# Two GpSimd operations per weight unit, and a first sub-layer put in another order

## What is computed

```python
mx = jnp.split((jax.nn.silu(c) @ mod_w[l] + mod_b[l])[:, None, :], N_MOD, axis=-1)
x = x + 0.5 * mx[2] * swiglu(modulate(rms_norm(x, norm_ffn1[l]), mx[0], mx[1]), ffn1_w_in[l], ffn1_w_out[l])
ux = modulate(rms_norm(x, norm_mix[l]), mx[3], mx[4])
yx, yh = token_mixer(ux, uh, w_in[l], ..., not last)
x = x + mx[5] * yx
x = x + 0.5 * mx[8] * swiglu(modulate(rms_norm(x, norm_ffn2[l]), mx[6], mx[7]), ffn2_w_in[l], ffn2_w_out[l])
```

## Time and profile before

| | |
|---|---|
| median of 3 executions | 2095.47 us |
| lowest and highest | 2094.98 and 2096.15 us |
| the profiled execution | 2095.26 us |
| its span in the trace | 2093.5 us |
| mean granted clock of TensorE | 0.983 |
| TensorE busy | 2016.0 us (96%) |
| GpSimd busy | 937.9 us (45%) |
| VectorE busy | 859.4 us (41%) |
| ScalarE busy | 672.1 us (32%) |
| moved by DMA | 278.89 MB, 133 GB/s in the mean |

### The profile page before, as it was taken

How to read it: one execution, slowest core, us unless ns; L and a number is a source line. 1 busy time by engine, 2 the same in 40 slices (tenths; PEclk the granted TensorE clock), 3 DMA queues, 4 the chain that set the end, 5 groups by cost and what they waited for, 6 DMA issues and landing times.

```text
span 2093.5 us, 30142 instructions
## 1 busy us (share of the span) xinstructions
PE 2016.0 (96%) x10678; PEld 1646.4 (79%) x10678; DVE 859.4 (41%) x1320; ACT 672.1 (32%) x1063; POOL 937.9 (45%) x423
## 2 busy tenths in 40 slices
PE   4899999999999999999999999999999899989998
PEld 2677777887667888878877887788778777989998
DVE  5323123438763124633123345322334775574313
ACT  3222222234453223421222243222223444444333
POOL 2244434453112443344434344444434433867886
PEclk7999999999999999999999999999999999999999
DMA  8354665243112333444455235534533522655564
GB/s 288 126 189 134 215 202 168 69 107 120 45 41 60 90 100 91 131 160 150 121 161 167 71 114 162 181 108 141 170 112 93 145 76 66 180 151 151 165 181 127
DMA packets 436977, 278.89 MB, mean 133 GB/s; under 512 B 25219, under 2 KB 398461, under 8 KB 436653
## 3 DMA queue, kind: packets, MB, share of 16 engines
q1 hardware_dynamic: 401868, 206.79, 33.5%
q10 hardware_dynamic: 34944, 71.05, 9.6%
q0 software_dynamic: 96, 0.16, 0.0%
HBM read 276.92 MB, written 1.05 MB: 133 GB/s over the span
## 4 chain that ended last, share of the span: by engine, by line
PE 82%; issue 7%; DVE 5%; POOL 4%; DMA 1%; ACT 1%; ACTq 0%; POOLq 0%; SPq 0%; DVEq 0%
PE bank L1194 25%; PE bank L1195 24%; PE bank L1196 24%; POOL w_lo L421 4%; PE bank L1264 3%; DVE u_lo L866 1%; PE bank L1515 1%; PE bank L1450 1%; PE bank L1272 1%; PE bank L1497 1%; DVE tmp L853 1%; DMA tok_rows<-in_ctx 0%; PE bank L1397 0%; DMA dft_tok<-in_c_dft_tok 0%; DVE rstd L1024 0%
## 5 line engine op out<-in xcount | busy, mean ns | idle before, releaser
L421 POOL TENSOR_TENSOR w_lo<-w_raw,w_hi 128x1024 fp32r<-128x1024 f32 (+2 forms) x412 | 935.3, 2285 | 1143.1 <-ACT w_hi L453 1143.1
L1194 PE MATMUL bank<-u_hi,w_hi 128*128 128x512 f32 (+1 forms) x2016 | 739.5, 367 | 23.8 <-DVE u_lo L866 20.9
L1195 PE MATMUL bank<-u_lo,w_hi 128*128 128x512 f32 (+1 forms) x2016 | 725.8, 360 | 0.0
L1196 PE MATMUL bank<-u_hi,w_lo 128*128 128x512 f32 (+1 forms) x2016 | 725.1, 360 | 0.0
L1194 PEld LDWEIGHTS bank<-u_hi,w_hi 128*128 128x128 f32 x2016 | 385.1, 191 | 105.7 <-issue 41.4
L453 ACT ACTIVATE w_hi<-w_raw 128x1024 fp32r<-128x1024 f32 (+2 forms) x412 | 385.6, 968 | 172.5 <-PE bank L1196 167.1
L1196 PEld LDWEIGHTS bank<-u_hi,w_lo 128*128 128x128 f32 x2016 | 384.7, 191 | 57.5
L1195 PEld LDWEIGHTS bank<-u_lo,w_hi 128*128 128x128 f32 x2016 | 385.3, 191 | 54.9 <-issue 1.4
L911 DVE TENSOR_TENSOR hf<-bank,sg 128x512 f32<-128x512 f32 (+1 forms) x85 | 53.2, 626 | 579.7 <-ACT sg L548 579.7
L1194 PE MATMUL bank<-h_hi,w_hi 128*128 128x512 f32 (+1 forms) x704 | 257.3, 366 | 3.6 <-DVE x L895 3.1
L548 ACT ACTIVATE sg<-bank 128x512 f32<-128x512 f32 (+1 forms) x85 | 46.3, 545 | 653.0 <-PE bank L1196 652.8
(11 more groups left out here) (149 smaller groups left out, 1594.7 us busy)
## 6 DMA issues: line engine op xcount, KB each, us to landing
w_raw<-in_ffn_w_in SPq DMA_DIRECT2D x176, 512.0 KB, 3.8
mod_w<-in_mod_w ACTq DMA_DIRECT2D x64, 1024.0 KB, 7.3
w_raw<-in_w_in SPq DMA_DIRECT2D x68, 512.0 KB, 3.7
w_raw<-in_ffn_w_out SPq DMA_DIRECT2D x64, 384.0 KB, 3.4
w_raw<-in_ffn_w_out SPq DMA_DIRECT2D x64, 320.0 KB, 3.3
mod_first<-in_mod_w SPq DMA_DIRECT2D x4, 2048.0 KB, 14.1
w_raw<-in_w_o SPq DMA_DIRECT2D x16, 512.0 KB, 3.9
w_raw<-in_w_in SPq DMA_DIRECT2D x16, 256.0 KB, 3.8
```

Of the source, the lines that this page charges most:

```text
L421: pool.tensor_tensor(w_lo[:, slot, 0:n, :], w_raw[:, slot, 0:n, :], w_hi[:, slot, 0:n, :].bitcast(F32), ALU.subtract).then_inc(S("w_lo_rea ...
L1194: pe.matmul(dst, w_hi[:, slot, kk, :], hi_[:, ka, 0:n], start=start, stop=False)
L1195: pe.matmul(dst, w_hi[:, slot, kk, :], lo_[:, ka, 0:n], start=False, stop=False)
L1196: return pe.matmul(dst, w_lo[:, slot, kk, :], hi_[:, ka, 0:n], start=False, stop=stop)
```

## The change

1. GpSimd makes each remainder in two operations, chunks 0 to 3 and the rest, and w_lo_ready counts two per unit. TensorE waits for the first at chunk 0 and for the second at chunk 4. The waits of the loads are rewritten for the new count.
2. At the start, the mean square is taken from the rows as they were loaded: ScalarE squares each row block of 128 tokens with a sum over its 1024 channels (four operations, with u_lo as scratch). The eight squares, eight additions and the mean-square matmuls there go. All later counts of ssq_added, sq_ready and ms_ready shift by one norm.
3. SP loads group 0, units 0 and 1, group 1, units 2 and 3, then groups 2 and 3.
4. ScalarE splits units 0 and 1 before it copies the first rounds, and units 2 and 3 in the middle of `norm(0)`, one ahead of each copy.
5. TensorE turns six chunks, runs the first round, turns the last two (now into banks 0 to 2), spreads, and runs the second round. The first two pairs are taken by halves of chunks in `start_pairs`: first half of pair 0 with rounds three and four between its chunks, first half of pair 1, second half of pair 0, the next group's round, second half of pair 1.
6. `columns_norm` handles both modulation vectors in one operation: three operations for six, and no chain semaphore behind the first.
7. A loop body is peeled in ScalarE's and VectorE's lists where the new count would be zero.

```diff
@@ -327,7 +329,7 @@
             slot, g, _ = ph.at(j, c, i, per)
-            wait(sp, S("w_lo_ready"), g - RING + 1)
+            wait(sp, S("w_lo_ready"), (g - RING + 1) * 2)
             for p0, p1, k0, k1, src in srcs:
...
@@ -335,10 +337,15 @@
             sp.dma_start(mod_first[:, g], t["mod_w"][0].rearrange("(k p) c -> p k c", p=P)[:, :, MG * g:MG * g + MG]).then_inc(first_loaded[G], 16)
-        for G in range(2):
-            load_first(G)
-        for j in range(2):
-            load(phases[order[0]], [(0, P, 0, DC, t["ffn1_w_in"][0].rearrange("(k p) c -> p k c", p=P)[:, :, j * D_FF:j * D_FF + P])], j, 0, 0, 2)
+        def load_early(c):
+            for j in range(2):
+                col = j * D_FF + c * P
+                load(phases[order[0]], [(0, P, 0, DC, t["ffn1_w_in"][0].rearrange("(k p) c -> p k c", p=P)[:, :, col:col + P])], j, c, 0, 2)
+
+        load_first(0)
+        load_early(0)
+        load_first(1)
+        load_early(1)
         for G in range(2, N_START):
...
@@ -418,8 +425,9 @@
             pool.wait_ge(S("w_hi_ready"), g + 1)
-            pool.tensor_tensor(w_lo[:, slot, 0:n, :], w_raw[:, slot, 0:n, :], w_hi[:, slot, 0:n, :].bitcast(F32),
-                               ALU.subtract).then_inc(S("w_lo_ready"), 1)
+            for k0, k1 in ((0, LO_SPLIT), (LO_SPLIT, n)):
+                pool.tensor_tensor(w_lo[:, slot, k0:k1, :], w_raw[:, slot, k0:k1, :], w_hi[:, slot, k0:k1, :].bitcast(F32),
+                                   ALU.subtract).then_inc(S("w_lo_ready"), 1)
         for key in order:
...
@@ -493,6 +501,7 @@
                     for G in range(2, N_START):
+                        hi(phases[order[0]], G - 2, 1)
                         copy_mod(G)
...
@@ -609,14 +618,16 @@
                        ACT.Silu).then_inc(S("sil_ready"), 1)
-        for d in range(DC):
-            square_at(d, d, d % 2, d, TOK)
-        root_of(0)
+        for a in range(2 * TT):
+            act.wait_ge(rows_loaded[a // TT], 16)
+            act.activation(u_lo[:, 2 * a:2 * a + 2, :].rearrange("p a n -> p (a n)"), tok_rows[:, a, :], ACT.Square,
+                           accum_out=row_sq[:, a:a + 1]).then_inc(S("row_sq_done"), 1)
+        act.wait_ge(S("ones_set"), 3)
+        act.wait_ge(S("row_sq_done"), 2 * TT)
+        act.activation(root[:, 0:2 * TT], row_sq[:], ACT.Sqrt, bias=eps_col[:, 0:1], scale=1.0 / D).then_inc(S("root_ready"), 1)
+        first_hi(order[0])
         for G in range(2):
             copy_mod(G)
-        first_hi(order[0])
-        for j in range(2):
-            hi(phases[order[0]], j, 1)
         norm(0)
...
@@ -794,14 +805,14 @@
             l, w = k // 3, k % 3
+            b0, b1 = 3 * DC * w + d0, 3 * DC * w + d1
+            a0, a1 = b0 + DC, b1 + DC
+            both = lambda cols: cols.unsqueeze(1).to_broadcast([P, 2, d1 - d0])
             gain = vec[:, l, V_N1 + DC * w + d0:V_N1 + DC * w + d1]
-            for v in range(2):
-                b0, b1 = 3 * DC * w + d0, 3 * DC * w + d1
-                a0, a1 = b0 + DC, b1 + DC
-                link(dve.tensor_tensor(colB[:, k, v, d0:d1], modcol[:, l, v, b0:b1], vec[:, l, b0:b1], ALU.add))
-                link(dve.tensor_tensor(colA[:, k, v, d0:d1], modcol[:, l, v, a0:a1], vec[:, l, a0:a1], ALU.add))
-                link(dve.scalar_tensor_tensor(out=colA[:, k, v, d0:d1], in0=colA[:, k, v, d0:d1], scalar=1.0, in1=gain,
-                                              op0=ALU.add, op1=ALU.mult))
+            dve.tensor_tensor(colB[:, k, :, d0:d1], modcol[:, l, :, b0:b1], both(vec[:, l, b0:b1]), ALU.add)
+            link(dve.tensor_tensor(colA[:, k, :, d0:d1], modcol[:, l, :, a0:a1], both(vec[:, l, a0:a1]), ALU.add))
+            link(dve.scalar_tensor_tensor(out=colA[:, k, :, d0:d1], in0=colA[:, k, :, d0:d1], scalar=1.0, in1=both(gain),
+                                          op0=ALU.add, op1=ALU.mult))
             if k:
...
@@ -985,10 +996,7 @@
             dve.wait_ge(S("x_turned"), d + 1)
-            dve.tensor_copy(x[:, d, :], bank[:, 4 + d % 3, :]).then_inc(S("x_done"), 1)
-            if d:
-                add_squares(d - 1, (d - 1) % 2, TOK)
-        add_squares(DC - 1, (DC - 1) % 2, TOK)
+            dve.tensor_copy(x[:, d, :], bank[:, d % 3, :]).then_inc(S("x_done"), 1)
         def start_columns(h):
...
@@ -1182,9 +1190,10 @@
             slot, g, _ = ph.at(j, c, i, per)
-            pe.wait_ge(S("w_lo_ready"), g + 1)
             nk = ph.kd[j]
             for kk in range(nk):
+                if kk in (0, LO_SPLIT):
+                    pe.wait_ge(S("w_lo_ready"), g * 2 + (2 if kk else 1))
                 if k_wait:
...
@@ -1223,10 +1234,6 @@
                         spread(k)
-                if first and k == 0 and kk == DC // 2 - 1:
-                    for G in range(2, N_START):
-                        mod_rounds(G)
-                        mod_turn(G)
             if early:
...
@@ -1237,9 +1244,42 @@
                         spread(k)
+        def start_pairs(n):
+
+            ph = phases[order[0]]
+
+            def half_pair(c, kk0, between=()):
+                slots = []
+                for j in range(2):
+                    slot, g, _ = ph.at(j, c)
+                    pe.wait_ge(S("w_lo_ready"), g * 2 + (2 if kk0 else 1))
+                    slots.append(slot)
+                for kk in range(kk0, kk0 + DC // 2):
+                    pe.wait_ge(S("u_ready"), kk + 1)
+                    for j, s in enumerate(slots):
+                        last = three(bank[:, 2 * c + j, 0:n], s, kk, u_hi, u_lo, kk, n, kk == 0, kk == DC - 1)
+                        if kk == DC - 1:
+                            last.then_inc(S("w_used"), 1)
+                    for step in between[kk - kk0:kk - kk0 + 1]:
+                        step()
+
+            def second_round():
+                mod_rounds(2)
+
+            def third_round():
+                mod_turn(2)
+                mod_rounds(3)
+
+            half_pair(0, 0, (lambda: None, second_round, third_round, lambda: mod_turn(3)))
+            half_pair(1, 0)
+            half_pair(0, DC // 2)
+            mod_rounds(BG_BASE[0, 1])
+            half_pair(1, DC // 2)
+            mod_turn(BG_BASE[0, 1])
+
         def mean_square(k):
-            pe.wait_ge(S("ssq_added"), DC * (k + 1))
+            pe.wait_ge(S("ssq_added"), DC * k)
             for a in range(norm_tokens(k) // P):
...
@@ -1331,21 +1374,22 @@
             for a in range(2 * TT):
-                last = pe.transpose(bank[:, 4 + d % 3, P * a:P * a + P], tok_rows[:, a, P * d:P * d + P], ident[:])
+                last = pe.transpose(bank[:, d % 3, P * a:P * a + P], tok_rows[:, a, P * d:P * d + P], ident[:])
             last.then_inc(S("x_turned"), 1)
         pe.wait_ge(S("vec_ready"), 1)
         pe.wait_ge(S("ones_set"), 3)
         pe.wait_ge(S("ones_r_set"), 1)
-        for d in range(DC):
+        for d in range(DC - 2):
             turn_x(d)
         pe.wait_ge(S("sil_ready"), 1)
-        mean_square(0)
-        for G in range(2):
-            mod_rounds(G)
-            mod_turn(G)
-            if G == 0:
-                spread(0)
+        mod_rounds(0)
+        for d in range(DC - 2, DC):
+            turn_x(d)
+        spread(0)
+        mod_turn(0)
+        mod_rounds(1)
+        mod_turn(1)
         for l in range(DEPTH):
```

More of the change, by code:

```diff
@@ L600, in body @@
                         if half == 1:
[L601 removed]
+                            square_at(m0 + c + i * 2, DC * (nxt - 1) + c + i * 2, c, c + i * 2, norm_tokens(nxt))
                             if nxt < 6:
                                 first_scaled(nxt, c, i)
[L604 removed]
+                turns(act, DC // 2 - 1, body, peel=half == 1 and nxt == 1)
                 body(DC // 2 - 1, tail=True)
@@ L974, in body @@
                         mod_extract(G, *mod_plan(l, f, G))
-                turns(dve, DC // 2 - 1, body)
+                turns(dve, DC // 2 - 1, body, peel=half == 1 and nxt == 1)
                 body(DC // 2 - 1)
@@ L1292, in body @@
                 def body(i):
+                    if half == 0 and not k and isinstance(i, int):
+                        start_pairs(n)
+                        return
                     with_mods = mods and not (half == 0 and k and isinstance(i, int))
```

28 lines of the change are left out of this document (15 added, 13 removed).

## The result

The changed kernel took 2056.6 us in the median of three executions (2056.4 to 2059.7), against 2095.22 for the kernel before, timed on the same chip: a ratio of 0.982, 95% interval 0.980 to 0.984. A fourth execution, at a mean granted clock of 0.556, took 3344.9 us and is left out of this and of the ratio; with it the median would be 2058.16. The forecast was 2058, range 2050 to 2073. Five more executions later gave 2057.6 (2053.1 to 2060.6), ratio 0.982 (0.980 to 0.983).

A forecast was written before the change was run, and what follows sets the result against it. TensorE, busy 96% of the span, was taken as the bound, so only its idle time and slow clock could be won: 2095.3 - 23.6 (start) - 14 (halves) = 2057.7, said as 2058 us, range 2050 to 2073.

The forecast's parts named there:

- The start: Before the first layer's products: first product at 33.2 against 49.5, second pair's end at 65.5 against 89.1, gain 23.6 us.
- The halves: GpSimd remainders in two operations: VectorE's waits halve, mostly in the last 450 us; gain 14 us, bounds 1 and 18.
- (a): Gates at 1953 to 1963 us: h_lo and four colG operations shorten, TensorE's wait and low clock go; 4.3 us.
- (b): Layer 1's output projection: VectorE's two waits delay x, ScalarE's next split and TensorE; 4.5 of 5.4 us gained.
- (c): Last chunks of a norm: u_lo and its like wait for GpSimd while TensorE idles, at three norms; 3.3 us gained.
- (d): Two single blocked operations ahead of TensorE waits of 2 us; 1.3 us gained.
- (e): Three waits of 0.2 to 0.4 us in the last phase; 0.6 us gained.
- GpSimd's price: Each remainder operation's fixed part of 0.18 us, paid 412 times more: 74 us more GpSimd busy time, hidden under TensorE's.
- the halves win nothing: Rival, chance 0.15: GpSimd keeps VectorE out for both pieces, or ScalarE closes the chain behind 1850 us; 2070 us.
- only the earlier first half counts: Same rival of useless halves, chance 0.15: TensorE's earlier start on a unit is the only gain, 1 to 2 us.
- The rival on the transfers: Start, chance 0.15: early units delay group 1's landing to near 30, everything behind shifts by 4.6; 2062 us.
- That GpSimd becomes the bound: Units of 256 tokens, last 340 us, chance 0.03: halves of 1.9 us make the kernel slower, 2153 us.

The follow-up runs named there:

- e5_splits_late: The changed kernel with ScalarE's first four splits behind both copies again; second pair's silu at 67.04 us, 2.8 later; one execution.
- e1_whole: The changed kernel with one whole GpSimd remainder operation per unit, new start kept; 2073.71 us, ratio 0.989.
- e0_after: The changed kernel itself, run once more with nothing altered; 2057.62 us, ratio 0.982.
- e2_halves: The kernel before with only the GpSimd remainders cut into halves, old start kept; 2080.10 us, ratio 0.993.
- e3_wait_both: The changed kernel, but TensorE waits for both remainder halves before a unit's first product; 2059.65 us, ratio 0.984.

## Why the prediction was right, by its own steps

**The start: 23.6 forecast, 24.46 measured.** First product at 33.35 (33.2), second round at 25.69 (25.5), third column at 30.27 (30.3), end of the second pair at 64.6 (65.5). The one piece that VectorE has to wait for is there, at the diagonal, but it is not what held the second round: group 1's weights landed at 25.56 (25.4 forecast), together with the end of the turn, and e5_splits_late shows that without the piece the round begins no sooner. The forecast had both at the same time, so the number holds whichever came last. Nearly all of the last 0.9 is the clock: over 33 to 40 us it is granted 0.76, so low for about 3.4 us or eight products of 0.43, and I had given it twelve. The term hangs on several steps at once: undone singly, the splits cost 2.8, the loads 3.5, the additions 5.8 and the order of pairs 7.8, which is 19.9; whether they add was not tested.

**The halves: 14 forecast, 14.2 measured behind the start in the profiled execution** (38.7 - 24.5), 15.3 against e1_whole. The sum came out better than its terms, and in part by luck. The forecast's 14 were 12.8 of waits and 1.2 of low clock, in (a). The runs show 8 to 9 us less idle time and 5 to 8 us less busy time for the same products (e1_whole, above): waits were priced too high and the clock too low. By term, as steps of the lead: (a) the gates 4.8, from 32.3 to 37.1 (4.3 forecast); (b) the output projection 4.4, from 27.1 to 31.5 (4.5 forecast; 3.0 in e0_after); (c) and (d), norms and single operations, 2.6 up to the output projection and 0.9 behind it, 3.5 for 4.6 forecast; (e) 1.6 for 0.6. The mechanism of (a) is shown: every profile with halves gains 4.7 or 4.8 at the gates, e1_whole nothing; and in the output projection what u_lo waits for a piece falls from 2.1 to 1.0, half the piece and half the wait. That of (b) is as written in the view, but its size is not shown to be the halves': e1_whole's lead grows by 3.0 over the same stage (20.6 to 23.6), e2_halves' by 2.3, e3_wait_both's by 0.1, so against e1_whole the halves bring 1.4 there, and the agreement with 4.5 is luck in part. (c) is the mis-sized term. In layer 1's norm the waits on u_lo moved to other chunks and did not go (3.4 to 3.7 in the view of waits). (c) and (d) together are 4.0 in layer 0 less 1.4 in layer 1's mixers, where a spell of low clock fell in the changed kernel alone; 2.5 of the 4.0 are waits that went or shrank (below). (e) comes from the earlier first half, since e3_wait_both loses 0.9 there.

**GpSimd's price.** 74 more busy time forecast, 1011.6 - 937.9 = 73.7 measured, and the half's mean of 1.37 holds some of VectorE's turns.

**The rivals.** That the halves win nothing falls with e1_whole and e2_halves, and that only the earlier first half counts, with e3_wait_both. The Trainium skill (SBUF — State Buffer, "SBUF: two separate sides") has the lock held for a whole instruction, and the traces agree, with u_lo at 2.62 beside wholes of 2.4 and at 1.51 beside halves of 1.43. Were the next turn always GpSimd's, VectorE would not have got in once in the row of 14 at 1828 us, and it did at every unit. The rival on the transfers was half right. Group 1 was indeed issued at 14.24, behind the two early units, and its landing does set the second round, but at 25.56 and not near 30, so nothing shifted by 4.6. That GpSimd becomes the bound was priced by a half of 1.58; it measured 1.37 with VectorE's turns in it. Yet the rival had a neighbour that I had not seen: a GpSimd row without a gap that keeps VectorE out for 15 to 18 us. With halves it occurs in no run here, with quarters in both that use them at 256 tokens. The forecast's sentence that VectorE gets in between two queued operations was read from one place; it holds for wholes and halves here, and for quarters mostly, but not always.

## What to carry to other kernels

Where one engine's operations hold up another's, as GpSimd's do VectorE's here, cut the long operation of the engine with spare time: the other's waits shrink with the piece, and the fixed part (0.18 here) is the price. Stop cutting before the cutting engine's time per unit comes up to the pace of the engine that it feeds: at 2.8 against 2.88 VectorE was shut out twice for 15 to 18 us. Why is open, so look for single short operations that last many times their length. At a start, ask of each engine's list which entry stands ahead of the one that the chain needs: four small moves cost 3 to 8 us each when undone. And when a sum of waits comes out right, compare TensorE's idle time as well as the whole time: here it fell by less than the sum, and the clock made up the rest.

## What the runs showed that I had not expected

**The lock-out**: 15.28 to 18.22 us for VectorE operations of 0.29 and 0.42, twice in each of two kernels, at the same cast and the same addition both times; the cause of the choice is open.

**Spells of low clock fall differently for the same work.** Stretches of the kernel before at layer 0's mixers and at its second norm, then nearly the same work in the changed kernel (length, busy times with counts for TensorE, weight loads, VectorE, ScalarE and GpSimd, granted clock, DMA share, GB/s):

```profile
565.00:570.00 5.00, 5.00 (x22) 2.71 (x20) 2.43 (x8) 1.23 (x5) 0.00 (x0) 0.50 0.00 0
860.00:870.00 10.00, 10.00 (x48) 8.94 (x48) 9.75 (x23) 7.18 (x16) 2.40 (x1) 0.68 0.25 75
```

```profile
541.00:546.00 5.00, 5.00 (x30) 2.97 (x27) 3.71 (x11) 1.52 (x6) 0.00 (x0) 1.00 0.11 33
830.00:840.00 10.00, 10.00 (x60) 8.47 (x59) 8.01 (x21) 4.96 (x11) 2.94 (x3) 1.00 0.36 106
```

TensorE is busy throughout in all four, at the low level (0.50) in the first, for part of the time in the second, at the high level in the others. Other executions have such spells at one place, at both, or at a third. Each is worth some 1 to 3 us, so terms under 2 us of this forecast can't be judged from one pair of profiles. They also have to be looked for on both sides. From 423 to 572 us the lead climbs from 24.5 to 27.2, and the first row above seems to explain it; but the changed kernel has a spell too in this stretch, at 451 to 457 us of its own time, so the clock costs both about the same. The climb is waits: on pT 2.9 for 4.6, on the first u_lo and the squares none for 0.8. From there to 28.5 near 890 it is the spell of the second row, less 1.3 of waits that are new.
